# Dense matmuls whose moving operand is read from its last column to its first

## The chip, the cores and the metric

The kernel runs on one core of one Trainium2 chip. The metric is device time in microseconds (us) for one execution. A measurement of this kernel can tell a change of about 0.2% from no change.

## The reference

One transformer layer for 256 tokens of width 2048, all in float32. A condition vector gives nine shifts, scales and gates (`mod`). Then come a gated feed-forward block, a mixer (sliding-window attention and a chunked mLSTM side by side, with their projections), a second feed-forward block, and a final norm. Cut to what matters:

```python
mod = silu(c) @ w_ada + b_ada                       # 2048 x 18432
u = modulate(rmsnorm(h, norm1_g), sh1, sc1)
h = h + 0.5 * gt1 * swiglu(u, ffn1_w_in, ffn1_w_out)   # 2048 x 11264, 5632 x 2048
u = modulate(rmsnorm(h, norm2_g), sh2, sc2)
h = h + gt2 * hybrid_mixer(u, ..., w_in, w_att_up, w_mlstm_up, w_out)
u = modulate(rmsnorm(h, norm3_g), sh3, sc3)
h = h + 0.5 * gt3 * swiglu(u, ffn2_w_in, ffn2_w_out)
return rmsnorm(h, final_g)
```

## The kernel before, in words

TensorE multiplies in the four-byte type float32r, which keeps fewer bits than float32. To get float32 accuracy each weight and each activation is split into a high part and a low part, and three products are summed: high times high, high times low, and low times high. The activations are the stationary operand (`a_hi`, `a_lo`: 128 features by 128 tokens, loaded as weights of the array), the weights of the model are the moving operand (`hi`, `lo`: 128 rows by 512 columns, streamed through). The sum lands in PSUM, in one bank of 512 float32 per partition and per half of the tokens.

The weights come in chunks: one DMA of 1 MB from SyncE (SP) fills `raw`, 128 x 4 x 512, in a ring of four. A chunk is two units of two k tiles each. For each unit ScalarE (ACT) copies `raw` to `hi`, which rounds it (`split`, line 1047), VectorE (DVE) writes `raw - hi` to `lo`, in the place of `raw` (line 1471), and TensorE runs the unit (`unit`, from line 603): it waits once for `lo_done`, then for each of the two k tiles and each of the two token tiles (`tt`) issues the three matmuls of lines 614, 616 and 617 into the same bank `ps`, and the last one of the unit counts up `unit_used`, for which ACT waits before it overwrites `hi`, and SP before it loads over `raw` and `lo`.

All dense layers go through `unit`, in this order: first feed-forward block (three parts of 4, 4 and 3 column groups, each an "in" phase and an "out" phase), `proj`, `rest` (the only one with fewer columns, 264), `gates`, `up`, `wout`, and the second feed-forward block. The accumulators are `pa` and `pb`, two banks each; while one is filled, ACT and DVE empty the other. The vector-matrix product for `mod` is done beside all this, by DVE with weights of its own DMAs (`ada_w`, `ada_s`). The order on each engine is written out by hand and is joined by semaphores.

TensorE also runs other matmuls that don't go through `unit`: transposes, attention, mLSTM, and sums over partitions in plain float32 (line 678).

Of the kernel before, what the change touches and what calls it, by code (L numbers as in the profile page):

```python
# [35 lines left out]
RING = 4  # L36
# [21 lines left out]
def build(nc, x, c, positions, w_ada, b_ada, norm1_g, ffn1_w_in, ffn1_w_out, norm2_g, w_in,  # L58
# [126 lines left out]
    with ExitStack() as ctx:  # L185
        def sb(name, shape, dt=F32):
            return ctx.enter_context(nc.sbuf_tensor(name, shape, dt))
# [12 lines left out]
        lo = sb("lo", [P, RING, 4, NC], F32R)  # L200
        hi = sb("hi", [P, RING, 2, NC], F32R)
# [400 lines left out]
        def _(pe):  # L602
            def unit(ph, i, j, half, k0, n, a_hi, a_lo, bank, start, stop, w=NC, on=False, tts=(0, 1)):
                u = 2 * (ph.c0 + ph.per * i + j) + half
                if half == 0 and 0 in tts:
                    fold_rows(u // 2)
                pe.wait_ge(lo_done, u + 1)
                for kk in range(n):
                    w_hi = hi[:, (2 * j + half) % 4, kk, 0:w]
                    w_lo = lo[:, j % RING, 2 * half + kk, 0:w]  # L610
                    for tt in tts:
                        tok = slice(tt * P, (tt + 1) * P)
                        ps = bank[:, tt, 0:w]
                        pe.matmul(ps, a_hi[:, k0 + kk, tok], w_hi, start=start and kk == 0, stop=False,  # L614
                                  skip_group_check=on)
                        pe.matmul(ps, a_hi[:, k0 + kk, tok], w_lo, start=False, stop=False, skip_group_check=on)  # L616
                        mm = pe.matmul(ps, a_lo[:, k0 + kk, tok], w_hi, start=False,  # L617
                                       stop=stop and kk == n - 1, skip_group_check=on)
                if 1 in tts:
                    mm.then_inc(unit_used, 1)  # L620
                return mm
# [11 lines left out]
            def fold_rows(cidx):  # L633

                for f, row in enumerate(FOLDED):
                    if row_end[row] != cidx - 2:
                        continue
                    pe.wait_ge(consts, 9)
                    pe.wait_ge(fold_ok, f + 1)
                    pe.wait_ge(mod_ok, QUARTERS + f)  # L640
                    pe.wait_ge(gt_ok, 8 if row_end[row] > plan["wout"].c0 else 4)
                    pe.matmul(pm[:, 0:ADA_W // 32], fold_sel[:, :], fsum[:, :], start=True, stop=True)\
                        .then_inc(flushed, 1)
# [64 lines left out]
            def norm_units(ph, n):  # L708

                norm_row(n, 0)  # L710
                pe.wait_ge(h_ok, H_BLOCKS[n] + 4)
                h_turn(n, 6)
                h_turn(n, 7)
                for piece, (g, tts) in enumerate(PIECES[:4]):
                    if piece == 1:
                        norm_row(n, 1)
                    pe.wait_ge(nt_lo, 10 * (n - 1) + piece + 1)
                    unit(ph, 0, 0, g, 2 * g, 2, act_hi, act_lo, pa, g == 0, False, tts=tts)

            def in_body(ph, i, first, nat, norm=0, step=None):  # L720

                if not (isinstance(i, int) and i + ph.a0 == 0):
                    pe.wait_ge(pa_free, ph.a0 + i)
                if norm:
                    norm_units(ph, norm)
                for n_, (j, half, k0, n) in enumerate(units(8, 4)):
                    if n_ == 8:
                        if nat and not first:
                            transposes(ph.nat0 + i - 1)

                        if not nat:
                            pe.wait_ge(pb_free, ph.b0 + i)
                        elif first and ph.b0 > 0:
                            pe.wait_ge(pb_free, ph.b0)
                    if step:
                        step(n_)
                    if norm and n_ < 2:
                        continue
                    if norm and n_ < 8:

                        pe.wait_ge(nt_lo, 10 * (norm - 1) + n_ + 3)
                    unit(ph, i, j, half, k0 % KD, n, act_hi, act_lo, pa if n_ < 8 else pb, n_ % 8 == 0, n_ % 8 == 7)

            def out_phase(ph, kn, nat_last, gate=None, norm=0):
                last = list(units(4, kn))[-2:]
                for b in range(4):
# [6 lines left out]
                    for j, half, k0, n in units(4, kn):  # L753
                        if (b, j, half) == (1, 1, 0) and gate == 1:
                            gate_rows(gate, (2, 3))
                        if (b, j, half) == (2, 2, 0) and gate == 2:
                            gate_sums(gate, (2, 3))
                        if gate == 0 and (b, j, half) in ((0, 1, 0), (1, 2, 0), (3, 0, 0)):
                            gate_sums(gate, (b - b // 2,))
                        if b == 0 and k0 <= 4 * (kn - 1) < k0 + n:  # L760

                            pe.wait_ge(nat_lo, 2 * (nat_last + 1))
                        if norm and b > 0 and (j, half) == (2, 0):
                            pe.wait_ge(h_ok, H_BLOCKS[norm] + b)
                            h_turn(norm, 2 * b - 2)
                            h_turn(norm, 2 * b - 1)
                        if norm and b == 3 and j == 3:
                            if half == 0:
                                for tt in range(TT):
                                    for j_, half_, k0_, n__ in last:  # L770
                                        mm = unit(ph, b, j_, half_, k0_, n__, hid_hi, hid_lo, bank, False,
                                                  k0_ + n__ == 4 * kn, tts=(tt,))
                                    if tt == 0:
                                        mm.then_inc(tt_done, 1)
                            continue
                        unit(ph, b, j, half, k0, n, hid_hi, hid_lo, bank, (j, half) == (0, 0),
                             k0 + n == 4 * kn)
                        if b == 0 and (j, half) == (0, 1):
                            transposes(nat_last)
# [1425 lines left out]
```

## Time and profile before

| | us |
|---|---|
| time before, median of 3 runs | 2148.63 |
| the runs, lowest to highest | 2146.76 to 2148.84 |
| the profiled execution's own time | 2149.22 |
| its span, first to last instruction | 2147.1 |
| TensorE matmul busy | 2097.2 (98%) |
| TensorE weight load busy | 1732.0 (81%) |
| VectorE busy | 1509.1 (70%) |
| ScalarE busy | 1005.0 (47%) |

The profile shows one execution. PE is TensorE's matmul, PEld its weight load, which overlaps it. A matmul's own duration includes the time in which it fills and leaves the array, so that durations of successive matmuls overlap; what a matmul costs in a stream is the distance between its start and the next one's start (here called the pitch). The granted clock says which share of full speed the throttle gave TensorE.

### The profile page before, as it was taken

The numbers are of one execution on the slowest core, as the hardware profiler recorded it, in microseconds if no ns is written. First come the engines' busy times: TensorE is split into PE (matmuls) and PEld (weight loads), VectorE is DVE, ScalarE is ACT, GpSimd is POOL, SyncE is SP. The second block draws the span as 40 slices with busy tenths as digits, with TensorE's granted clock in tenths as the row PEclk, the third lists the DMA queues.
The fourth block names the chain that finished last, engine by engine and source line by source line (L and its number), as shares of the span: only waits on it lengthen the run. The fifth ranks groups of instructions, "written<-read, shape, count | busy, mean of one in ns | idle before, by whom it ended". The sixth has DMA issues, their size and how long they took to land.

```text
span 2147.1 us, 23938 instructions
## 1 busy us (share of the span) xinstructions
PE 2097.2 (98%) x9531; PEld 1732.0 (81%) x9531; DVE 1509.1 (70%) x1694; ACT 1005.0 (47%) x1276; POOL 4.2 (0%) x21
## 2 busy tenths in 40 slices
PE   5999999999999999999999999999999999999997
PEld 5778788888888878888888887878888888888886
DVE  6887997888788888786555789577555544555455
ACT  4566433443334455447555644454443444433443
POOL 0000000000000000000000000000000000000000
PEclk9999999999999999999999999999999999999998
DMA  9998898997898868865444688558655555555554
GB/s 340 386 372 287 316 332 311 332 337 273 311 333 330 284 219 320 315 235 173 155 156 156 235 287 313 204 206 300 218 179 193 196 185 187 194 192 190 189 172 142
DMA packets 248559, 539.70 MB, mean 251 GB/s; under 512 B 11520, under 2 KB 13824, under 8 KB 247808
## 3 DMA queue, kind: packets, MB, share of 16 engines
q1 hardware_dynamic: 248448, 538.17, 71.1%
q8 instruction: 75, 1.23, 0.2%
q14 instruction: 36, 0.29, 0.0%
HBM read 536.03 MB, written 2.10 MB: 251 GB/s over the span
## 4 chain that ended last, share of the span: by engine, by line
PE 86%; DVE 3%; ACT 1%; issue 1%; DMA 0%; DVEq 0%; ACTq 0%
PE pa L614 14%; PE pb L614 14%; PE pa L617 14%; PE pa L616 14%; PE pb L617 14%; PE pb L616 14%; PE px L629 1%; DVE lo L1471 1%; ACT hi L1047 0%; DVE ada_acc L1560 0%; PE px L697 0%; PE pr L931 0%; PE px L938 0%; PE pm L930 0%; DMA raw<-in_w_in_dram 0%
## 5 line engine op out<-in xcount | busy, mean ns | idle before, releaser
L1471 DVE TENSOR_TENSOR lo<-raw,hi 128x1024 fp32r<-128x1024 f32 (+1 forms) x744 | 882.0, 1195 | 551.1 <-ACT hi L1047 550.4
L1047 ACT CAST hi<-raw 128x1024 fp32r<-128x1024 f32 (+1 forms) x744 | 761.8, 1028 | 1002.2 <-PE pa L617 495.5
L614 PE MATMUL pa<-hi,act_hi 128*128 128x512 f32 (+1 forms) x1056 | 415.8, 394 | 7.2 <-DVE act_lo L1852 3.2
L617 PE MATMUL pa<-hi,act_lo 128*128 128x512 f32 (+1 forms) x1056 | 409.6, 388 | 0.0
L616 PE MATMUL pa<-lo,act_hi 128*128 128x512 f32 (+1 forms) x1056 | 409.5, 388 | 0.0
L614 PE MATMUL pb<-hi,act_hi 128*128 128x512 f32 x1024 | 403.0, 394 | 0.0
L617 PE MATMUL pb<-hi,act_lo 128*128 128x512 f32 x1024 | 398.7, 389 | 0.0
L616 PE MATMUL pb<-lo,act_hi 128*128 128x512 f32 x1024 | 398.6, 389 | 0.0
L1560 DVE SCALAR_TENSOR_TENSOR ada_acc<-ada_w,cond,ada_acc 128x1024 f32<-128x1024 f32 (+1 forms) x240 | 275.4, 1147 | 6.0
L614 PEld LDWEIGHTS pa<-hi,act_hi 128*128 128x128 f32 x1056 | 199.5, 189 | 52.0 <-DVE act_lo L1613 4.4
L617 PEld LDWEIGHTS pa<-hi,act_lo 128*128 128x128 f32 x1056 | 199.3, 189 | 41.3
L616 PEld LDWEIGHTS pa<-lo,act_hi 128*128 128x128 f32 x1056 | 199.8, 189 | 39.0 <-issue 0.2
L617 PEld LDWEIGHTS pb<-hi,act_lo 128*128 128x128 f32 x1024 | 192.2, 188 | 40.3
L614 PEld LDWEIGHTS pb<-hi,act_hi 128*128 128x128 f32 x1024 | 192.3, 188 | 39.9 <-issue 1.3
L616 PEld LDWEIGHTS pb<-lo,act_hi 128*128 128x128 f32 x1024 | 192.4, 188 | 38.7
L614 PE MATMUL pb<-hi,hid_hi 128*128 128x512 f32 x416 | 164.1, 394 | 0.0
L614 PE MATMUL pa<-hi,hid_hi 128*128 128x512 f32 x416 | 164.1, 394 | 0.0
L617 PE MATMUL pa<-hi,hid_lo 128*128 128x512 f32 x416 | 162.0, 390 | 0.0
L617 PE MATMUL pb<-hi,hid_lo 128*128 128x512 f32 x416 | 162.0, 389 | 0.0
L616 PE MATMUL pa<-lo,hid_hi 128*128 128x512 f32 x416 | 161.9, 389 | 0.0
L616 PE MATMUL pb<-lo,hid_hi 128*128 128x512 f32 x416 | 161.8, 389 | 0.0
L614 PEld LDWEIGHTS pb<-hi,hid_hi 128*128 128x128 f32 x416 | 78.1, 188 | 17.1 <-issue 1.0
(278 smaller groups left out, 1334.9 us busy)
## 6 DMA issues: line engine op xcount, KB each, us to landing
raw<-in_ffn_w_in_dram SPq DMA_DIRECT2D x176, 1024.0 KB, 4.9
ada_w<-in_w_ada_dram SPq DMA_DIRECT2D x224, 512.0 KB, 6.0
raw<-in_ffn_w_out_dram SPq DMA_DIRECT2D x64, 1024.0 KB, 5.1
raw<-in_w_in_dram SPq DMA_DIRECT2D x64, 1024.0 KB, 5.1
ada_s<-in_w_ada_dram SPq DMA_DIRECT2D x64, 512.0 KB, 8.8
raw<-in_ffn_w_out_dram SPq DMA_DIRECT2D x32, 768.0 KB, 4.4
raw<-in_w_out_dram SPq DMA_DIRECT2D x16, 1024.0 KB, 5.1
raw<-in_w_att_up_dram SPq DMA_DIRECT2D x8, 1024.0 KB, 5.1
```

Source lines behind the costliest of these rows:

```text
L614: pe.matmul(ps, a_hi[:, k0 + kk, tok], w_hi, start=start and kk == 0, stop=False, skip_group_check=on)
L616: pe.matmul(ps, a_hi[:, k0 + kk, tok], w_lo, start=False, stop=False, skip_group_check=on)
L617: mm = pe.matmul(ps, a_lo[:, k0 + kk, tok], w_hi, start=False, stop=stop and kk == n - 1, skip_group_check=on)
L629: mm = pe.transpose(px[:, b, ft * T + tt * P:ft * T + (tt + 1) * P], buf_b[:, tt, (2 * b + ft) * P:(2 * b + ft + 1) * P], ident[:, :])
L1047: act.copy(hi[:, (2 * j + half) % 4, 0:n, 0:w], raw[:, j % RING, 2 * half:2 * half + n, 0:w])\
L1471: dve.tensor_tensor(lo[:, j % RING, s, 0:w], raw[:, j % RING, s, 0:w], hi[:, (2 * j + half) % 4, 0:n, 0:w].bitcast(F32), ALU.subtract)\
L1560: ins = dve.scalar_tensor_tensor(out=acc, in0=wt, scalar=cond[:, kt:kt + 1], in1=acc, op0=ALU.mult, op1=ALU.add)
```

## The change

In `unit`, the moving operands and the output take a reversed access pattern: the start is the last column, the step is minus one element. Column 511 of the weights is multiplied first, and its result is written first, to column 511 of the bank, so that every result lies where it lay. The stationary operands, the number and the order of instructions, the waits, the DMAs and everything outside `unit` are as they were. In the program as it is built, the matmuls of `unit` carry a start offset larger by 511 (263 in `rest`) and an innermost step of -1 on the moving operand and on the output.

```diff
@@ -606,11 +606,11 @@
                     fold_rows(u // 2)
                 pe.wait_ge(lo_done, u + 1)
                 for kk in range(n):
-                    w_hi = hi[:, (2 * j + half) % 4, kk, 0:w]
-                    w_lo = lo[:, j % RING, 2 * half + kk, 0:w]
+                    w_hi = hi[:, (2 * j + half) % 4, kk, 0:w][:, ::-1]
+                    w_lo = lo[:, j % RING, 2 * half + kk, 0:w][:, ::-1]
                     for tt in tts:
                         tok = slice(tt * P, (tt + 1) * P)
-                        ps = bank[:, tt, 0:w]
+                        ps = bank[:, tt, 0:w][:, ::-1]
                         pe.matmul(ps, a_hi[:, k0 + kk, tok], w_hi, start=start and kk == 0, stop=False,
                                   skip_group_check=on)
                         pe.matmul(ps, a_hi[:, k0 + kk, tok], w_lo, start=False, stop=False, skip_group_check=on)
```

## Rows read from the trace of the kernel before

**Rows 1.** The page: the granted clock and DMA share in 40 slices, and the chain.

```profile
PEclk9999999999999999999999999999999999999998
DMA  9998898997898868865444688558655555555554
...
PE 86%; DVE 3%; ACT 1%; issue 1%; DMA 0%; DVEq 0%; ACTq 0%
```

**Rows 2.** The waits: who waited for whom, us in total, times, longest us.

```profile
DVE lo L1471 <- ACT hi L1047: 550.4, 454, 5.4
ACT hi L1047 <- PE pa L617: 495.5, 309, 3.5
ACT hi L1047 <- PE pb L617: 479.3, 307, 3.5
```

**Rows 3.** Groups of TensorE by form: xcount | busy us, mean ns | idle before.

```profile
L614 PE MATMUL pa<-hi,act_hi 128*128 128x512 f32 x1024 | 406.7, 397 | 7.2 <-DVE act_lo L1852 3.2 <-DVE act_lo L1613 2.3 <-DVE act_lo L1529 1.7
L614 PE MATMUL pb<-hi,act_hi 128*128 128x512 f32 x1024 | 403.0, 394 | 0.0
...
L614 PE MATMUL pb<-hi,hid_hi 128*128 128x512 f32 x416 | 164.1, 394 | 0.0
L614 PE MATMUL pa<-hi,hid_hi 128*128 128x512 f32 x416 | 164.1, 394 | 0.0
...
L614 PE MATMUL pa<-hi,act_hi 128*128 128x264 f32 x32 | 9.1, 285 | 0.0
```

**Rows 4.** Order of time, second feed-forward block: start us, us, engine, instruction.

```profile
1700.22 0.39 PE L614 MATMUL pb<-hi,act_hi 128*128 128x512 f32 x1
1700.22 0.19 PEld L616 LDWEIGHTS pb<-lo,act_hi 128*128 128x128 f32 x1
1700.44 0.39 PE L616 MATMUL pb<-lo,act_hi 128*128 128x512 f32 x1
1700.67 0.39 PE L617 MATMUL pb<-hi,act_lo 128*128 128x512 f32 x1
...
1707.70 0.39 PE L614 MATMUL pb<-hi,act_hi 128*128 128x512 f32 x1
```

**Rows 5.** Order of time, TensorE, the first dense matmuls of the program.

```profile
41.93 0.63 PE L617 MATMUL pa<-hi,act_lo 128*128 128x512 f32 x1
42.36 0.63 PE L614 MATMUL pa<-hi,act_hi 128*128 128x512 f32 x1
...
46.20 0.63 PE L614 MATMUL pa<-hi,act_hi 128*128 128x512 f32 x1
46.63 0.44 PE L616 MATMUL pa<-lo,act_hi 128*128 128x512 f32 x1
```

**Rows 6.** Order of time, TensorE, in `rest`, where the operands have 264 columns.

```profile
975.95 0.28 PE L614 MATMUL pa<-hi,act_hi 128*128 128x264 f32 x1
...
978.83 0.28 PE L614 MATMUL pa<-hi,act_hi 128*128 128x264 f32 x1
```

**Rows 7.** Order of time, TensorE, sums in plain float32 (x2: merged records).

```profile
1635.22 1.02 PE L678 MATMUL pr<-ada_acc,ones 128*128 128x512 f32 x2
1636.08 1.02 PE L678 MATMUL pm<-ada_acc,ones 128*128 128x512 f32 x2
```

**Rows 8.** Stages: length, busy us (records) of PE, PEld, DVE, ACT, POOL, clock, DMA share, GB/s.

```profile
60.00:200.00 140.00, 136.06 (x608) 110.58 (x607) 119.06 (x126) 93.47 (x124) 0.00 (x0) 1.00 0.98 356
1650.00:2130.00 480.00, 480.00 (x2148) 398.11 (x2147) 248.35 (x220) 200.83 (x215) 0.00 (x0) 1.00 0.55 186
```

## The prediction

> **What bounds the kernel now.** I read the page first, then the waits, the groups by form, the order of time, and last two stages side by side.
>
> The chain of work that ended last is TensorE's for 86% of the span, with DMA at 0%, and the granted clock stands in its top tenth in all slices but the last [rows 1]. The waits say the same from the other side: VectorE waits 550 us in total for ScalarE's copies, and ScalarE waits 495.5 + 479.3 = 975 us for TensorE to finish with a buffer [rows 2]. The two engines that prepare the weights are ahead of TensorE and are held back by it. The reader should see there that TensorE is waited for and hardly waits.
>
> What TensorE does in that time is a stream of equal matmuls. Line 614 runs 1024 + 1024 + 416 + 416 = 2880 times with 512 columns and 32 times with 264 [rows 3]; lines 616 and 617 run as often, so there are 8640 wide ones and 96 narrow ones. A duration of 394 ns is no cost per matmul, since durations overlap. The pitch is the cost: from 1700.22 to 1707.70 us lie 33 matmuls, 7.48 / 33 = 0.2267 us each, and inside one group of three the starts are as evenly spaced as two decimals can show [rows 4]. The weight load of the next matmul takes 0.19 us, starts with the present one and is over before the next begins [rows 4]. So 8640 x 0.2267 = 1959 us, and the narrow ones, 24 of them in 978.83 - 975.95 = 2.88 us [rows 6], give 96 x 0.120 = 12 us. Together that is 1970 of 2147.1 us, 92% of the span. The rest is the start, the end and other matmuls, which the change doesn't touch.
>
> Two more rows say what the pitch is made of. At the start, at the lower of the two clock levels, ten matmuls take 46.20 - 41.93 = 4.27 us, 0.427 us each [rows 5], which is 512 columns at 1.2 GHz. Half of that is 0.2133, so the pitch at 2.4 GHz is the time of the columns and 13.3 ns more. With 264 columns it is 0.120 us, of which the columns are 264 x 0.2133 / 512 = 0.110, and about 10 ns are left [rows 6]. So most of the surcharge comes once per matmul, not per column.
>
> **The change, part by part.** It removes nothing, adds nothing and moves nothing. All three engines and SP have the same instructions, in the same order, with the same waits.
>
> *What is waited for.* No consumer looks at single columns. `unit` waits for the whole of `lo`, and ACT, DVE and SP wait for the last matmul of a unit or a phase. That the columns appear in another order inside a matmul lets nobody start sooner or later: 0 us. Both banks have been read and released by a semaphore before the next matmul opens them, so there is no early overwriting of a part either.
>
> *Successive matmuls into one bank.* The three matmuls of a group, and those of the following k tiles, add onto the same columns. Column c is written again one pitch later, whether all go up or all go down, since every writer of `pa` and `pb` on TensorE is turned round together: 0 us.
>
> *The stationary operand.* It isn't reversed. Its 0.19 us [rows 4] stay beside the previous matmul: 0 us. If the pitch rose, they would be hidden the better.
>
> *The rate at which columns are read and written.* This is the only term that is open: 8640 x (new pitch - 0.2267), and next to all of it on the path, since ScalarE and VectorE have 975 and 550 us of waiting in hand [rows 2] and a slower TensorE would only give them more. No row of this trace reads or writes backwards, so the price is bounded from both sides. From above: a plain float32 matmul of 512 columns takes 1636.08 - 1635.22 = 0.86 us [rows 7], which is what would be paid if a reversed operand lost the fast path of float32r altogether; nearer, one column per tick of 1.2 GHz is 0.427 us [rows 5]. From below: the whole surcharge of 13.3 ns could go, which would be 8640 x 0.0133 = 115 us. The value I take is 0. The neighbours of the reversed stream are the same neighbours, two steps in a row touch adjacent words as before, and the rate at 2.4 GHz is one column per clock with a surcharge that counts matmuls and not columns [rows 4 to 6], which looks like an address that is stepped, by whatever amount, and not like a block that is fetched upwards. That is an argument from likeness and not a measurement, and the whole risk of the prediction is in it.
>
> This term is judged very finely. About 0.2% is what a measurement of this kernel can tell from no change, 4.3 us, and 4.3 / 8640 is 0.5 ns of pitch.
>
> The trace shows full rate only for ascending, contiguous operands [rows 4]. The Trainium skill has a rule against this change: "Advanced Engine Details and Errata", section PSUM Cachelines, says that PSUM works in lines of two float32 and that an access pattern that isn't contiguous slows matmuls much. Read strictly, by it a step of -1 is not contiguous and the sum would be the second rival's; read by its next sentence, that every two consecutive elements should be contiguous, columns 511 and 510 still share a line and the sum stays at 0. The same page, section 2x-1p Requirements, lets a step of -1 count as a unit step for VectorE; nothing here shows it for TensorE.
>
> The sum against the profiled execution: 2149.22 + 0 = 2149.2 us, which lies 0.6 above the median of the runs. For the median I forecast 2148.6.
>
> **The rivals.**
>
> *A small surcharge per matmul (slower).* One mechanism: a reversed access needs a few ticks more to begin or to close, at the place where the 13.3 ns stand now. One tick of 1.2 GHz is 0.427 / 512 = 0.83 ns [rows 5], which makes 7 us in 8640 matmuls, 2156 in all; a surcharge twice as large as now makes 115 us, 2264. It decides from 0.5 ns on. For it: a surcharge exists, and nothing in the rows shows its cause. Against it: it was the same for all bank changes and all three lines, so it doesn't seem to hang on the pattern.
>
> *Half rate (slower).* Two columns are read or written per tick of the slower clock now, as a pair, and the pair is only formed upwards. Then the pitch is 0.427 us [rows 5], and the time is 2149 + 8640 x 0.200 + 96 x 0.100 = 2149 + 1728 + 10 = 3887 us. For it: at the lower level the surcharge is gone and at the higher it isn't [rows 4, 5], so something beside the array runs at its own pace. Against it: a pair of neighbours is a pair in both directions. A case between (two pairs of three, say) would lie between 2264 and 3887.
>
> *The plain price (slower).* The fast path of float32r is lost: 2149 + 8640 x 0.633 = 7618 us and some 30 more for the narrow ones. Only a check of the format for a step of exactly one would do that.
>
> *A shorter pitch (faster).* The surcharge shrinks, by at most 115 us, to 2034. But the first feed-forward block could not follow all the way: in 60 to 200 us the DMA engines are busy for 0.98 of the time and VectorE for 119 of 140 us; late in the program there is room, with a DMA share of 0.55 [rows 8]. A quarter of the surcharge, 29 us, is as far as I go: 2120. Nothing in the rows speaks for it.
>
> That the change doesn't do what it says is no rival, since the built matmuls carry the step of -1.
>
> **How the numbers follow.** No change: 0.64. Small surcharge: 0.13. Half rate, with the cases near it: 0.14. Plain price: 0.04. Shorter pitch: 0.05. So faster is 0.05, same 0.64, slower 0.31. The likeliest case gives 2148.6, and its own range is 2144 to 2153. To leave out no more than 2 in 10 the range has to take in the small surcharge, up to 2265, and the likelier half of the shorter pitch, down to 2120: 0.64 + 0.13 + 0.03 = 0.80. Half rate and the plain price are left out.
>
> **What would show it.** In the changed kernel the same stretch of the second feed-forward block should show starts 0.2267 us apart, durations of 394 ns on line 614, weight loads of 0.19 us, the first matmuls 0.427 us apart, ScalarE's waits for TensorE near 975 us in total and the stage from 1650 to 2130 in its place. I am wrong if the pitch differs by 0.5 ns or more. If only the narrow and the wide matmuls grow by the same amount each, it is the surcharge; if they grow in proportion to their columns, it is the rate. In a slower case ScalarE's wait for TensorE must grow by about the whole difference.

## The result, and the profile after

The changed kernel takes 2198.78 us (median of 4 runs, 2198.44 to 2200.18) against 2148.73 us of the kernel before: ratio 1.0236, 95% interval [1.0221, 1.0252]. It is slower by 50 us. The profiled execution has a span of 2198.2 us, 51.1 more than before; its mean granted clock is 0.995, against 0.994 before, so the clock has no part in the loss.

First the pitch, where the prediction said to look: the order of time on TensorE in the second feed-forward block (start us, us, engine, instruction).

```profile
1735.02 0.40 PE L616 MATMUL pb<-lo,act_hi 128*128 128x512 f32 x1
1735.02 0.19 PEld L617 LDWEIGHTS pb<-hi,act_lo 128*128 128x128 f32 x1
1735.25 0.40 PE L617 MATMUL pb<-hi,act_lo 128*128 128x512 f32 x1
1735.48 0.40 PE L614 MATMUL pb<-hi,act_hi 128*128 128x512 f32 x1
...
1744.82 0.40 PE L616 MATMUL pb<-lo,act_hi 128*128 128x512 f32 x1
```

From 1735.02 to 1744.82 lie 42 matmuls, 9.80 / 42 = 0.2333 us each, against 0.2267 in [rows 4]. The weight load takes 0.19 us as before. At the lower clock level nothing has changed, and neither has the pitch of the narrow matmuls of `rest`, which run at the higher one. Here are two of the first matmuls of the program and two of `rest`, and then a stage inside those first ones, whose granted clock, the third number from the end, is 0.50:

```profile
41.23 0.63 PE L617 MATMUL pa<-hi,act_lo 128*128 128x512 f32 x1
...
45.07 0.54 PE L617 MATMUL pa<-hi,act_lo 128*128 128x512 f32 x1
...
998.93 0.28 PE L616 MATMUL pa<-lo,act_hi 128*128 128x264 f32 x1
...
1003.25 0.28 PE L616 MATMUL pa<-lo,act_hi 128*128 128x264 f32 x1
```

```profile
41.90:45.00 3.10, 3.10 (x8) 2.40 (x8) 2.98 (x5) 2.39 (x4) 0.00 (x0) 0.50 0.99 321
```

Nine matmuls in 45.07 - 41.23 = 3.84 us make 0.427 us, as in [rows 5], and 36 narrow ones in 4.32 us make 0.120, as in [rows 6]. So only the wide matmuls at the higher clock have become dearer, by 6.7 ns, which is 8 ticks of 1.2 GHz (0.83 ns each). The waits of the changed kernel (who waited for whom, us in total, times, longest) answer to [rows 2]:

```profile
DVE lo L1471 <- ACT hi L1047: 597.0, 466, 5.4
ACT hi L1047 <- PE pa L617: 520.2, 312, 3.5
ACT hi L1047 <- PE pb L617: 505.0, 309, 3.5
```

ScalarE waits 1025.2 us for TensorE instead of 974.8, 50.4 more, and VectorE 47 more for ScalarE: the whole of the loss went through TensorE and turned up as waiting behind it. The busy times and the chain from the page:

```profile
PE 2149.5 (98%) x9531; PEld 1733.5 (79%) x9531; DVE 1510.6 (69%) x1694; ACT 1002.3 (46%) x1276; POOL 4.2 (0%) x21
...
PE 88%; DVE 2%; ACT 1%; issue 1%; DMA 0%; DVEq 0%; ACTq 0%
```

The other engines do the same work as before. Counted over the whole program, the distance between the starts of successive wide matmuls at the higher clock is 0.22705 us before (8391 distances) and 0.23335 after (8395), 6.3 ns apart: before, the six or so that follow an interruption stand near 0.23, so that the mean gap is a little smaller than 6.7. 8391 x 0.0063 = 52.9 us; the other 250 or so distances are at the lower clock or hold an interruption. From the start of the first wide matmul to that of the last it is 51.8 us more (2091.8 and 2143.6), and as the first one happened to start 0.7 us earlier in the changed kernel (40.21 against 40.91), the span grew by 51.1. The 1.1 us between 52.9 and 51.8 were not located.

### The profile page after: what moved, and what is told of

Read it like the earlier page. It is cut to its first block, busy times and chain, and to the rows that moved or that the text cites. A ratio compares the mean times of both kernels' runs of the same rounds, so it can differ in the third digit from the quotient of the medians.

```text
span 2198.2 us, 23938 instructions
## 1 busy us (share of the span) xinstructions
PE 2149.5 (98%) x9531; PEld 1733.5 (79%) x9531; DVE 1510.6 (69%) x1694; ACT 1002.3 (46%) x1276; POOL 4.2 (0%) x21
## 4 chain that ended last, share of the span: by engine, by line
PE 88%; DVE 2%; ACT 1%; issue 1%; DMA 0%; DVEq 0%; ACTq 0%
PE pa L614 14%; PE pb L614 14%; PE pb L616 14%; PE pb L617 14%; PE pa L617 14%; PE pa L616 14%; PE px L629 1%; DVE lo L1471 0%; PE px L697 0%; PE pr L931 0%; ACT hi L1047 0%; PE px L938 0%; DVE ada_acc L1560 0%; DMA raw<-in_w_in_dram 0%; PE pm L930 0%
## 5 line engine op out<-in xcount | busy, mean ns | idle before, releaser
L614 PE MATMUL pa<-hi,act_hi 128*128 128x512 f32 (+1 forms) x1056 | 423.3, 401 | 7.0 <-DVE act_lo L1852 3.2
L616 PE MATMUL pa<-lo,act_hi 128*128 128x512 f32 (+1 forms) x1056 | 417.6, 395 | 0.0
L617 PE MATMUL pa<-hi,act_lo 128*128 128x512 f32 (+1 forms) x1056 | 417.5, 395 | 0.0
L614 PE MATMUL pb<-hi,act_hi 128*128 128x512 f32 x1024 | 411.0, 401 | 0.0
L616 PE MATMUL pb<-lo,act_hi 128*128 128x512 f32 x1024 | 407.0, 397 | 0.0
L617 PE MATMUL pb<-hi,act_lo 128*128 128x512 f32 x1024 | 406.9, 397 | 0.0
```

## The experiments

Twelve kernels ran, eight of them versions of the layer. With each stands what was expected of it before it ran.

### Which operand

`e1_moving` leaves the output ascending, `e2_out` the moving operands:

```diff
 e1_moving, against the changed kernel
-                        ps = bank[:, tt, 0:w][:, ::-1]
+                        ps = bank[:, tt, 0:w]
 e2_out, against the kernel before
-                        ps = bank[:, tt, 0:w]
+                        ps = bank[:, tt, 0:w][:, ::-1]
```

> The moving operands are reversed, the output is not, so the columns of every dense product come out mirrored within their 512: the numbers of the layer are others, the work is the same. Theory A (the backward read from SBUF costs the extra time): the pitch of the 512-column matmuls is 0.2333 us as in the changed kernel, the time is about 2199 us. Theory B (the backward write to PSUM costs it): pitch 0.2267, time about 2149 us. Theory C (it takes both, or each carries half): something between, 2160 to 2190 us.

> Only the output is reversed; products come out mirrored within their 512 columns, the work is the same. Theory A (backward read): pitch 0.2267 us, about 2149 us. Theory B (backward write): pitch 0.2333 us, about 2199 us. Theory C: between, and the excess of this run and of the one with the moving operands alone add up to 50 us.

`e1_moving`: 2199.34 us, ratio to before 1.0235 [1.022, 1.025]. `e2_out`: 2148.18 us, 0.9998 [0.9989, 1.0008]. Counted as above, the mean distance of wide matmuls at the higher clock is 0.2334 us in the first and 0.2270 in the second. The waits of both, the first three rows of `e1_moving`:

```profile
DVE lo L1471 <- ACT hi L1047: 597.6, 469, 5.4
ACT hi L1047 <- PE pa L617: 520.5, 312, 3.5
ACT hi L1047 <- PE pb L617: 504.8, 308, 3.5
```

and of `e2_out`:

```profile
DVE lo L1471 <- ACT hi L1047: 550.6, 454, 5.4
ACT hi L1047 <- PE pa L617: 495.0, 309, 3.5
ACT hi L1047 <- PE pb L617: 478.4, 306, 3.5
```

The backward read from SBUF makes the whole difference; the backward write to PSUM costs nothing. The Trainium skill's rule that the prediction weighed ("Advanced Engine Details and Errata", PSUM Cachelines: a pattern that isn't contiguous slows matmuls much) did not bite on a step of -1; its next sentence, on pairs, is the one that these runs agree with, though none of them pulls the pairs of the output apart.

### TensorE by itself, kinds side by side

`m1_kinds` and its three successors leave out the layer: they load a few tiles and then let TensorE run alone, in stretches of equal matmuls (48 per kind in `m1_kinds`, 96 in the others). Each ran once; ascending kinds repeated at the end of a run read 226.8 to 227.1 ns where they had read 226.7, which is how finely these rows can be told apart. The three-way change of banks is that of the kernel. One kind is one line:

```python
for i in range(N):  # down 512
    pe.matmul(rev(O(i), 512), S(i), rev(W(i), 512), start=i % 24 < 4, stop=i % 24 == 23, skip_group_check=True)
```

`S(i)` walks through 16 stationary tiles, `W(i)` through four moving ones, `O(i)` changes the bank after every third. All tiles start at multiples of 64 elements (256 bytes) unless a kind says otherwise, as in the layer; below this is called the home place. "Up" is ascending, "down" descending.

> This kernel computes nothing of the layer: after one load it runs 43 kinds of matmul, 48 of each in a row, with nothing else on the chip, and stores its input with one accumulator in it. Each kind stands on a line of its own, so that its pitch can be read. Expected if the extra time is TensorE's own and not a clash with DMA, ScalarE or VectorE: 512 columns up 0.2267 us, down 0.2333 us, 264 columns 0.120 us both ways. Theory A (read): moving down alone 0.2333, output down alone 0.2267; theory B (write) the other way round. If pairs or lines of four must be formed upwards, blocks of 2 or of 4 that are ascending inside and descending among themselves go at 0.2267; if it is the order of large stretches, halves swapped cost too. If the extra is a clash of the moving read with the weight load beside it (both read SBUF), a stationary operand of 64 columns halves or removes it, and an offset of the moving operand by some elements moves it, up as well as down; if it is a fixed cost per reversed instruction, neither does. Over the widths 128 to 504 a fixed cost shows as equal steps between up and down, a rate as steps in proportion; the unchanged 264 speaks against both already.

TensorE's order of time, merged by line. The start of one kind's row less that of the row before, over 48, is the pitch of that row (L93 both down, L95 moving down, L97 output down, then L99 begins; an ascending kind ran before L93):

```profile
49.27 11.37 PE L93 MATMUL pa<-w_r,s_r 128*128 128x512 f32 x48
60.47 11.37 PE L95 MATMUL pa<-w_r,s_r 128*128 128x512 f32 x48
71.67 11.06 PE L97 MATMUL pa<-w_r,s_r 128*128 128x512 f32 x48
82.57 0.67 PE L99 MATMUL pa<-w_r,s_r 128*128 128x128 f32 x5
```

Both down 11.20 / 48 = 0.2333 us, moving down 0.2333, output down 10.90 / 48 = 0.2271. With nothing else running on the chip the numbers are those of the layer, so no other engine and no DMA has a part in it. Of the other kinds, worked out in the same way:

| kind | pitch, ns |
|---|---|
| 128 columns up / down | 110.6 / 111.5 |
| 192 up / down | 112.3 / 111.7 |
| 256 up / down | 120.4 / 118.3 |
| 264 up / down | 121.3 / 120.0 |
| 320 up / down | 146.7 / 146.7 |
| 384 up / down | 173.5 / 177.7 |
| 448 up / down | 202.7 / 206.5 |
| 504 up / down | 227.1 / 229.0 |
| 512 up / down | 226.7 / 233.3 |
| 512 with 64 stationary columns, up / down | 230.0 / 233.1 |
| blocks of 2 or 4 down, ascending inside | 233.3 |
| halves swapped (blocks of 256) | 227.1 |
| up, moving operand from element 32 / 64 / 128 / 256 on | 232.7 / 227.1 / 226.7 / 226.7 |
| up, moving operand from element 1 on | 236.9 |
| down, moving operand from 1 on | 235.6 |
| down, moving operand from 4, 16, 32, 64, 128, 256 on | 233.3 to 233.5 |
| moving step 2 / -2 | 450.8 / 466.7 |

At 128 and 192 columns the pitch hardly depends on the width. Above that, neither a fixed cost per reversed instruction nor a rate per column fits: at 256, 264 and 320 columns down is not dearer, and 512 columns up cost no more than 504. What stands out is the row on offsets: **an ascending read that starts 32 elements later costs as much as a descending one.** And two kinds in bf16, the second of which ends where the last row starts:

```profile
432.78 10.55 PE L169 MATMUL pa<-w_b,s_b 128*128 128x512 bf16 x48
443.17 10.52 PE L171 MATMUL pa<-w_b,s_b 128*128 128x512 bf16 x48
453.53 1.88 PE L173 MATMUL pa<-raw,h 128*128 128x512 f32 x4
```

In bf16 up takes 10.39 / 48 = 0.2165 us and down 0.2158: with half the bytes per column there is hardly a surcharge over 0.2133 and none for the direction. Plain float32 takes 0.858 us up and 0.850 down, so there too the direction costs nothing. The places of the operands were not varied in either format.

### Where the operands lie

> Again a kernel of TensorE alone, 38 kinds, 96 matmuls of each. Known: 512 columns up 0.2267 us, moving down 0.2333, halves swapped 0.227, blocks of 4 descending 0.2333, up from 32 elements on 0.2327. Theory K (clash: the moving read and the weight load beside it fall on the same part of SBUF at the same time): the pitch up and down changes when only the stationary operand is moved by 16 to 96 elements, 'both moved by 32' need not equal 'moving operand moved by 32', and fewer stationary columns change the surcharge, down to nearly none with 16. Theory R (the moving read alone: it pays for every block of SBUF that it enters, more so against the block's order): moving the stationary operand changes nothing, up at 64 and multiples 0.2267 and all other offsets dearer, and there is one block size b, between 8 and 128 elements, from which descending blocks cost as little as ascending ones. With one pair of addresses only, both theories expect the same pitch as the mean of many, unless the sixteen stationary addresses differ among themselves.

`m2_places` moves the stationary operand or the moving one (L95 down; L97, L99, L101 and L103 up with the stationary operand 16, 32, 48 and 64 elements on; 96 matmuls each):

```profile
72.12 22.57 PE L95 MATMUL pa<-w_r,s_r 128*128 128x512 f32 x96
94.53 22.57 PE L97 MATMUL pa<-w_r,s_r 128*128 128x512 f32 x96
116.93 22.48 PE L99 MATMUL pa<-w_r,s_r 128*128 128x512 f32 x96
139.24 22.14 PE L101 MATMUL pa<-w_r,s_r 128*128 128x512 f32 x96
161.22 21.94 PE L103 MATMUL pa<-w_r,s_r 128*128 128x512 f32 x96
183.00 1.33 PE L105 MATMUL pa<-w_r,s_r 128*128 128x512 f32 x5
```

That is 233.4 ns down, and up 233.3, 232.4, 229.0 and 226.9. The moving operand was not touched in these four; only its neighbour moved. With both 32 elements on it is 226.9 again. Blocks that descend among themselves cost 233.3 (8 elements), 233.4 (16), 232.3 (32), 226.8 (64) and 226.7 (128). Theory R fails on its first sign, since the stationary operand alone matters; its block size exists, and is 64. Of theory K that sign came true, but two others did not. Down stays at 233.3 with the stationary operand 16, 32 or 64 elements on. And with 16, 32, 96 and 112 stationary columns the pitch is 231.1, 231.7, 230.0 and 233.3 up, and 233.3 down with the first three: fewer columns loaded do not make the surcharge smaller.

The Trainium skill, "TensorE: Matmul & The Clock Gate", section Step-by-step: what each phase is for, says that TensorE has two independent read ports into SBUF and that loading the next weights takes no bandwidth from the running matmul. For this format at the higher clock the trace is hard to square with it: moving nothing but the stationary operand by 64 bytes costs 6.7 ns per matmul. That the two reads take bandwidth from each other is not shown by this, only that they are not independent.

Two runs of the layer carry this over.

```diff
 e3_halves, against the kernel before; the same on w_lo and ps
-                    w_hi = hi[:, (2 * j + half) % 4, kk, 0:w]
+                    w_hi = hi[:, (2 * j + half) % 4, kk, 0:w].rearrange("p (a b) -> p a b", a=2)[:, ::-1, :]
 e4_fours: b=4 in place of a=2
```

> The layer in full: each operand and output is taken as two halves of 256 columns (132 in the narrow phase), second half first, ascending inside. If the direction within a block of 256 is what costs, this runs at a pitch of 0.2267 us and in about 2149 us, although the access pattern is as little contiguous as a jump makes it; if any departure from one ascending run costs, 2199 us.

> The layer in full: blocks of 4 columns (16 bytes), ascending inside, the blocks from last to first, on the operands and the output. If the order of neighbours inside a line cost the time, this runs in about 2149 us; if it is the order of larger blocks, as the small kernel says (0.2333 us for such blocks), about 2199 us.

`e3_halves`: 2148.3 us, 0.9996 [0.9987, 1.0006]. `e4_fours`: 2198.54 us, 1.0234 [1.0217, 1.0251]. The mean distances are 0.2270 and 0.2334 us. Reading out of order is free in large blocks, and ascending inside a block of 16 bytes saves nothing when the blocks descend.

### The same loss without any reversal

```diff
 e5_shift16, against the kernel before; [P, 64] in e6_shift64; e7_down_shift16 has it in the changed kernel
         hi = sb("hi", [P, RING, 2, NC], F32R)
+        sb("shift", [P, 16])
         act_hi = sb("act_hi", [P, KD, T], F32R)
```

> The kernel before, nothing reversed; 64 unused bytes per partition stand before the stationary operands (and all that is allocated after them). Theory K: the pitch of the 512-column matmuls becomes 0.2333 us, and the time 2199 us, the same as of the change, without any backward read. Theory D: 2149 us. (Narrow matmuls may change too, they are 12 us in all.)

> The same with 256 unused bytes. Theory K: the placing modulo 256 bytes is as before, pitch 0.2267 us, 2149 us. If moving the tiles costs something else (DMA, ScalarE), this run shows it beside the one with 64 bytes.

> The changed kernel (operands and output reversed) with the 64 unused bytes. If the reversed read is at its dearest anyway: pitch 0.2333 us, 2199 us, both costs are one cost. If reversal and placing add up: 0.240 us, 2255 us.

`e5_shift16`: 2198.34 us, 1.0236 [1.0219, 1.0253], with this order of time (its lines stand one further down):

```profile
1735.51 0.40 PE L617 MATMUL pb<-lo,act_hi 128*128 128x512 f32 x1
...
1744.61 0.39 PE L617 MATMUL pb<-lo,act_hi 128*128 128x512 f32 x1
```

39 matmuls in 9.10 us, 0.2333 each. Sixty-four unused bytes cost as much as reading everything backwards, and like that only at the higher clock: the first wide matmuls of the program are 0.43 us apart here too. `e6_shift64`, with 256 bytes: 2148.87 us, 1.0003 [0.9993, 1.0012]. `e7_down_shift16`: 2199.35 us, 1.0237 [1.0222, 1.0253]: the two costs are one and do not add.

### Is there a lucky place for a descending read?

> TensorE alone, 38 kinds, 96 matmuls each. Found so far: up costs 272 ticks of 1.2 GHz (0.2267 us) only when stationary and moving operand start at the same place modulo 64 elements (256 bytes), up to 280 (0.2333) elsewhere; down cost 280 at every placing tried. Theory K (clash of the two reads): up with the stationary operand at 1 to 60 elements lies at 274 to 280; down may have its own lucky place among 1 to 60, then it goes to 272 there. Theory D (down is dear of itself, whatever lies beside it): 280 at all eight. A read that pays for itself: one of three down 229, two of three 231, every other 230 ns; if a change of direction costs, every other is the dearest. Accumulating into one bank or changing it each time: 226.7 and 233.3 as before, if the output has no part in it.

Here are down with the stationary operand at 56 (L123) and 60 (L125), then one (L127) and two (L129) of every three moving operands down, at the home place (start us, us):

```profile
384.75 22.56 PE L123 MATMUL pa<-w_r,s_r 128*128 128x512 f32 x96
407.14 22.88 PE L125 MATMUL pa<-w_r,s_r 128*128 128x512 f32 x96
429.86 22.15 PE L127 MATMUL pa<-w_r,s_r 128*128 128x512 f32 x96
451.85 22.57 PE L129 MATMUL pa<-w_r,s_r 128*128 128x512 f32 x96
474.26 1.09 PE L131 MATMUL pa<-w_r,s_r 128*128 128x512 f32 x4
```

Down is 233.2 to 233.4 ns at 1, 4, 8, 24, 40, 48 and 56, and 236.7 at 60: no lucky place. Up is 232.4 to 234.3 at 1, 4, 8, 24, 40 and 56, but 226.8 at 60, so a multiple of 64 elements was cheap wherever it was tried, and is not the whole rule. `m4_turns` below adds 226.7 at 54 and 226.8 at 63, and 231.1 to 233.2 at 52, 58, 59, 61 and 62. One of three down costs 229.1 (229 was expected of reads that each pay for themselves), every other one 230.1 (230), but two of three cost the full 233.4, not 231, and with one of three stationary operands 16 elements on it is 231.1: the costs of single matmuls do not simply add up. One bank throughout, or another bank each time, changes nothing (226.8, 226.9; down in one bank 233.3).

The series of `m2_places` that moves the moving operand instead, set beside the one that moves the stationary operand, shows what counts. It is how far the stationary operand starts beyond the moving one, modulo 64 elements; a moving operand 8 elements on makes that 56:

| stationary start beyond the moving one | by moving the stationary, ns | by moving the moving one, ns |
|---|---|---|
| 8 | 233.2 | 233.2 |
| 16 | 233.3 | 233.2 |
| 24 | 234.3 | 234.2 |
| 32 | 232.4 | 232.7 |
| 40 | 233.3 | 233.4 |
| 48 | 229.0 | 228.9 |
| 56 | 233.2 | 233.4 |

Even the odd values at 24 and 48 agree, so in steps of 8 elements an ascending pitch is set by the distance between the two starts. In finer steps it isn't: at 60 the two ways give 226.8 and 231.6, at 63 they give 226.8 and 236.9.

> TensorE alone, 37 kinds, 96 matmuls each. Open: which two reads stand in each other's way, and why down is dear at every placing. Theory N (neighbours: the moving read of one matmul and the weight load of the next, which runs beside it): with even matmuls both at 0 and odd ones both at 32 elements, every load runs beside a moving read of the other placing, so 279 ticks of 1.2 GHz; with stationary and moving at 0 and 32, then 32 and 0, load and read side by side match, 272. Theory O (own: a matmul's own weights and its own moving operand): the other way round, 272 and 279. If both matter, or it is a matter of starts and ends of the instructions, neither goes to 272. Few stationary columns (2 or 16) at their best placing: below 272 if the clash grows with the columns loaded, 272 or more if it is a matter of phase alone. Down: if it has a lucky place, one of the six new ones shows 272; blocks of 256 or 64 whose inside is descending while the blocks ascend show whether it is the direction inside a block (280) or of the whole (272).

The question of theory N and theory O came out neither way. In the rows, L97 has both operands at 0 and 32 in turn, L99 crosses them:

```profile
94.39 22.09 PE L97 MATMUL pa<-w_r,s_r 128*128 128x512 f32 x96
116.32 22.24 PE L99 MATMUL pa<-w_r,s_r 128*128 128x512 f32 x96
138.40 22.40 PE L101 MATMUL pa<-w_r,s_r 128*128 128x512 f32 x96
```

228.4 and 230.0 ns, where one of the two should have been 226.7 and the other 232.4; with 16 elements in place of 32 it is 231.7 and 231.8. Two stationary columns cost 231.7 at either of two places: the surcharge doesn't go below that of 128 columns at the home place. Down, at 12, 20, 28, 44 and 52, is 233.3, and 236.7 at 36; with the places of the kernels before, 28 placings of a descending read were tried and none was below 233. Blocks of 64 and of 256 that ascend while their inside descends cost 233.3 as well: the direction inside a block of 64 elements is what matters, not that of the whole.

One kind was a surprise: blocks of 32 elements, descending, cost 232.3 at home, but 227.3 with the stationary operand 32 elements on (L159), where plain ascending operands cost 232.4:

```profile
784.40 21.98 PE L159 MATMUL pa<-w_r,s_r 128*128 128x512 f32 x96
806.22 22.57 PE L161 MATMUL pa<-w_r,s_r 128*128 128x512 f32 x96
```

Order and place can cancel. The last run took that into the layer (wide operands only):

```diff
 e8_blocks32_shift32, against the kernel before
+        sb("shift", [P, 32])
         act_hi = sb("act_hi", [P, KD, T], F32R)
...
+            def turned(t, w):
+                return t.rearrange("p (a b) -> p a b", b=32)[:, ::-1, :] if w == NC else t
...
-                    w_hi = hi[:, (2 * j + half) % 4, kk, 0:w]
-                    w_lo = lo[:, j % RING, 2 * half + kk, 0:w]
+                    w_hi = turned(hi[:, (2 * j + half) % 4, kk, 0:w], w)
+                    w_lo = turned(lo[:, j % RING, 2 * half + kk, 0:w], w)
...
-                        ps = bank[:, tt, 0:w]
+                        ps = turned(bank[:, tt, 0:w], w)
```

> The layer in full. Wide operands and outputs go in blocks of 32 columns (128 bytes), last block first, ascending inside; and the stationary operands lie 128 bytes further on. The small kernels had such blocks at 278.8 ticks (0.2323 us) with the operands at the same place modulo 256 bytes and at 272.8 (0.2273) with the stationary one 128 bytes further on, while plain ascending operands with that shift had 278.9. If order and place act together, as two reads that meet or miss each other, this kernel has a pitch of about 0.227 us and runs in 2149 to 2156 us, though each of its two edits alone would cost some 48 us. If each departure costs by itself, 2195 us or more.

2146.19 us, ratio 0.999 [0.9981, 1.0]. Its order of time:

```profile
1700.18 0.39 PE L618 MATMUL pb<-hi,act_hi 128*128 128x512 f32 x1
...
1707.66 0.39 PE L618 MATMUL pb<-hi,act_hi 128*128 128x512 f32 x1
```

33 matmuls in 7.48 us, 0.2267, the pitch of [rows 4]. The 0.1% below the kernel before is within what can be told from no change. What each of the two edits costs alone in the layer was not run; the 48 us of the expectation come from the small kernels. No float32r kind in any of the four small kernels had a surcharge for 512 columns below the 13.3 ns of the kernel before, so there was no version to run that could have beaten it clearly.

## Why the prediction was wrong

**What bounds the kernel** held: 8640 wide matmuls at their pitch, everything else behind them. That is why 6.3 ns became 50 us, and why ScalarE's wait for TensorE grew by 50.4 us, as was said for a slower case.

**The steps at 0 us** (waits, successive matmuls into one bank) held: the output down alone gives 0.9998, and the bank changes make no difference.

**The stationary operand** is where the working was blind. The prediction put it at 0 us, since it isn't reversed and its 0.19 us stay beside the previous matmul. Its duration did stay. But where it lies relative to the moving operand decides 6.7 ns of the pitch with nothing reversed, and the prediction had no term for that. That the reversal costs its time by changing this relation is argued from `e7_down_shift16` and `e8_blocks32_shift32`, and not shown.

**The rate term** ("the rate at which columns are read and written") is the step that failed. It was put at 0, and the runs show 6.7 ns per wide matmul in a steady stretch, 6.3 in the mean, all of it from the read of the moving operand. The 0 came from the likeness that the surcharge "counts matmuls and not columns" and looks like an address that is stepped by whatever amount. From 264 and 512 columns a per-instruction surcharge of 10 to 13 ns was read. The widths between show that this was two lucky points: 384, 448 and 504 columns up have 13.5, 16.0 and 17.1 ns over their column time (width x 0.4167 ns), and 512 has 13.3; down they have 17.7, 19.8, 19.0 and 20.0. So the surcharge does grow with the columns, but not evenly; the kernel's 512 columns at multiples of 256 bytes sit in a dip, and the change left it. A trace in which every operand has the same order and the same place can't show how much of the pitch hangs on either.

**The rival "small surcharge"** had the sign and, with 2156 to 2264 us, the size (0.13 was its chance), but not the mechanism: it was to be a fixed cost of a reversed instruction, and then the narrow matmuls would have paid too. Neither of the two patterns that the prediction named, the same amount for every matmul or an amount in proportion to the columns, was seen. **Half rate** and **the plain price** did not come; half rate exists, for a moving step of 2 (450.8 ns), not for -1. The range of 2120 to 2265 held the time only because it had been stretched to take in that rival, and the forecast of no change, at 0.64, was too sure for a price that no row showed.

**What stays open.** Shown is this. The backward read of the moving operand makes the cost of the change, in float32r and not in bf16 or plain float32, and at 2.4 GHz and not at 1.2. The pitch of an ascending read depends on where the stationary operand lies relative to it. A displacement by 16 elements and the reversal cost the same and don't add. That the read of the moving operand and a weight load meet on some part of SBUF is the natural reading, and the table of distances speaks for it, but it is argued: the run that should have said which two reads meet gave values between, and loads of two columns cost as much as large ones. Why a descending read finds no lucky place isn't explained either.

## What to carry to other kernels

When TensorE streams float32r operands of 512 columns at 2.4 GHz, let stationary and moving tiles start at multiples of 256 bytes and read ascending within blocks of that size; a small tile that slips in before them can cost 3% of the pitch and 2.4% of a kernel like this, with nothing in the waits to show for it but a longer pitch. With both at such multiples, the order of blocks of 256 bytes or more is free, and so is the direction of the output. And before a stream of thousands of equal instructions is altered in any way, measure its pitch alone in a small kernel: 0.5 ns each is more than a forecast from likeness can promise.

## What was not expected of the hardware

- Ascending reads of 512 float32r columns take 226.7 ns or up to 236.9, by the place of the two operands alone; 512 columns cost no more than 504 (226.7 and 227.1).
- In steps of 8 elements that pitch follows the distance between the two starts modulo 256 bytes, whichever operand is moved: 229.0 and 228.9 at 48, 234.3 and 234.2 at 24.
- At 512 columns the pitch moves between a best value of 272 ticks of 1.2 GHz and 284, with 280 the commonest; bf16, at 260 up and 259 down, has no cost for the direction.
- A PSUM output with a step of -1 costs nothing: 0.9998 [0.9989, 1.0008].
- Two wrongs can make a right: descending blocks of 128 bytes and a shift of 128 bytes run at 226.7 ns together, in the layer.
